# Squares for the norms of queries and keys summed in single passes of TensorE, after GpSimd divides them into a rounded part and a remainder

## What is computed

```python
def l2norm(x):
    return x * lax.rsqrt(jnp.sum(x * x, axis=-1, keepdims=True) + EPS)

q = l2norm(qkv[..., :W].reshape(Bsz, S, H, Dh))
k = l2norm(qkv[..., W:2 * W].reshape(Bsz, S, H, Dh))
```

## Time and profile before

| | us |
|---|---|
| median of 3 runs | 2419.33 (2419.21 to 2419.52) |
| the profiled execution's own time | 2419.28 |
| its span, first to last instruction | 2417.6 |
| TensorE busy with matmuls | 2393.9 |
| VectorE busy | 1613.9 |
| ScalarE busy | 1165.9 |
| GpSimd busy | 158.0 |
| eight sums L1136, modelled length of the 16 entries together (16 x 0.593) | 9.5 |

### The profile page before, as it was taken

The page is one execution under the profiler, slowest core; times in us unless marked ns, Lnnn a source line. Parts: engine busy times, 40 slices in busy tenths (PEclk is TensorE's granted clock), DMA queues, the critical chain, the costliest instruction groups (busy, mean ns, idle before and its releaser), DMA issues.

```text
span 2417.6 us, 35323 instructions
## 1 busy us (share of the span) xinstructions
PE 2393.9 (99%) x14051; PEld 2069.5 (86%) x14051; DVE 1613.9 (67%) x2035; ACT 1165.9 (48%) x1404; POOL 158.0 (7%) x142
## 2 busy tenths in 40 slices
PE   8999999999999999999999999999999999999998
PEld 7888988888888888889988888888888888888887
DVE  6999676556675876697655445455777467755764
ACT  5433674545564654642654344345554344433433
POOL 1000000000200100000000000000222012200220
PEclk9999999999999999999999999999999999999999
DMA  8655446454435555653175554444655555555554
GB/s 250 196 187 196 153 139 226 137 190 157 159 117 195 169 179 176 191 158 106 40 262 177 184 201 147 146 167 145 203 192 190 198 185 187 195 188 195 181 178 144
DMA packets 337349, 422.43 MB, mean 175 GB/s; under 512 B 8494, under 2 KB 263228, under 8 KB 336716
## 3 DMA queue, kind: packets, MB, share of 16 engines
q1 hardware_dynamic: 334220, 410.87, 51.4%
q0 software_dynamic: 2544, 8.52, 1.1%
q10 hardware_dynamic: 464, 1.32, 0.2%
HBM read 418.53 MB, written 2.10 MB: 174 GB/s over the span
## 4 chain that ended last, share of the span: by engine, by line
PE 97%; DVE 2%; ACT 1%; DMA 0%; issue 0%; ACTq 0%; DVEq 0%
PE ps L747 36%; PE ps L748 18%; PE ps L806 10%; PE ps L804 10%; PE ps L805 10%; PE ps L751 1%; PE ps L750 1%; PE ps L752 1%; PE ps L1101 1%; PE ps L1093 1%; PE ps L1314 1%; PE ps L1015 1%; PE ps L1305 1%; PE ps L1018 1%; PE ps L843 0%; DVE h_cat L2285 0%
## 5 line engine op out<-in xcount | busy, mean ns | idle before, releaser
L747 PE MATMUL ps<-h_cat,w_hi 128*128 128x512 f32 x3824 | 1343.2, 396 | 5.6 <-DVE h_cat L2285 4.9
L748 PE MATMUL ps<-h_cat,w_lo 128*128 128x256 f32 x3824 | 1064.7, 278 | 0.0
L747 PEld LDWEIGHTS ps<-h_cat,w_hi 128*128 128x128 f32 x3824 | 716.9, 187 | 176.2 <-issue 7.5
L748 PEld LDWEIGHTS ps<-h_cat,w_lo 128*128 128x128 f32 x3824 | 719.9, 188 | 2.2 <-issue 1.9
L2142 DVE TENSOR_TENSOR w_lo<-ring,w_hi 128x2048 fp32r<-128x2048 f32 (+2 forms) x279 | 588.5, 2112 | 178.6 <-ACT w_hi L1395 175.8
L1395 ACT ACTIVATE w_hi<-ring 128x2048 fp32r<-128x2048 f32 (+2 forms) x279 | 493.1, 1768 | 86.4 <-PE ps L806 63.0
L2138 DVE TENSOR_TENSOR w_lo<-ring,w_hi 128x2048 fp32r<-128x2048 f32 (+1 forms) x136 | 303.1, 2233 | 230.2 <-ACT w_hi L1392 227.4
L1392 ACT ACTIVATE w_hi<-ring 128x2048 fp32r<-128x2048 f32 (+1 forms) x136 | 252.5, 1863 | 271.0 <-PE ps L806 250.4
L804 PE MATMUL ps<-w_hi,h_cat 128*128 128x512 f32 x640 | 250.6, 392 | 0.0
L806 PE MATMUL ps<-w_hi,h_cat 128*128 128x512 f32 x640 | 249.2, 389 | 0.0
L805 PE MATMUL ps<-w_lo,h_cat 128*128 128x512 f32 x640 | 249.0, 389 | 0.0
(11 more groups left out here) (439 smaller groups left out, 2262.6 us busy)
## 6 DMA issues: line engine op xcount, KB each, us to landing
ring<-in_w_ffn_up SPq DMA_DIRECT2D x44, 2048.0 KB, 8.0
ring<-in_w_mix_in SPq DMA_DIRECT2D x28, 2048.0 KB, 8.2
ring<-in_even_w_in SPq DMA_DIRECT2D x27, 2048.0 KB, 8.0
ring<-in_w_ffn_down SPq DMA_DIRECT2D x16, 2048.0 KB, 8.0
ring<-in_odd_w_in SPq DMA_DIRECT2D x11, 2048.0 KB, 9.2
ring<-in_even_w_out SPq DMA_DIRECT2D x8, 2048.0 KB, 8.1
ring<-in_odd_w_out SPq DMA_DIRECT2D x8, 2048.0 KB, 8.3
ring<-in_w_mix_out SPq DMA_DIRECT2D x8, 2048.0 KB, 8.3
```

What stands on the lines that cost most here:

```text
L747: mm(o[:, 0:2 * T], whi[slot][:, k, :], flat(cat[:, k]), start=first, stop=False)
L748: ins = mm(o[:, T:2 * T], wlo[slot][:, k, :], cat[:, k, 0, :], start=False, stop=end)
```

## The change

Each norm gets a step of GpSimd between square and sum. It casts the two halves of l2 into two tiles of the single-pass type, and subtracts them from l2 in place. TensorE waits for this step instead of the square. It sums the remainders (512 columns) and adds the rounded halves (256 columns each) in the same bank, with the ones taken as the single-pass type. One rounded half stands in 1 KB behind the delta rule's tiles, the other in the place of the tile rstd, which is not used then. ScalarE and VectorE are left as they are. The GpSimd steps are queued behind the masks and ahead of the load of L640.

```diff
-            add("act", "l2_square", s), add("pe", "l2_sum", s), add("act", "l2_root", s), add("dve", "l2_scale", s)
+            add("act", "l2_square", s), add("pool", "l2_split", s), add("pe", "l2_sum", s), add("act", "l2_root", s), add("dve", "l2_scale", s)
...
+    RSTD = at[0]
     rstd = place("rstd", [P, T])
...
     l2 = place("l2", [P, 2, T], off=XSQ)
+    l2_hi = [place("l2_hi0", [P, T], F32R, off=AR + 40 * KB), place("l2_hi1", [P, T], F32R, off=RSTD)]
+    l2_lo = place("l2_lo", [P, 2, T], F32R, off=XSQ)
...
+        def l2_split(s):
+
+            after(pool, "l2_square", s)
+            for i in range(2):
+                ch.link(pool.tensor_copy(l2_hi[i][:], l2[:, i, :]))
+            for i in range(2):
+                ins = pool.tensor_tensor(l2_lo[:, i, :], l2[:, i, :], l2_hi[i][:].bitcast(F32), ALU.subtract)
+                if i == 0:
+                    ch.link(ins)
+            return ins
+
+        for s in range(8):
+            l2_split(s).then_inc(sem["gdn_pool"], 1)
         pool.wait_ge(sem["h_ready"], H_GROUPS["gdn"] + 4)
...
         def l2_sum(s):
-            after(pe, "l2_square", s)
-            return mm(ps[4][:], ones[:], l2[:].rearrange("p a t -> p (a t)"), start=True, stop=True)
+            after(pe, "l2_split", s)
+            one = ones[:].bitcast(F32R)
+            mm(ps[4][:], one, flat(l2_lo[:]), start=True, stop=False)
+            mm(ps[4][:, 0:T], one, l2_hi[0][:], start=False, stop=False)
+            return mm(ps[4][:, T:2 * T], one, l2_hi[1][:], start=False, stop=True)
```

More of the change, by code:

```diff
@@ L402, in build @@
              "idx_ready", "relu_ready", "idx_added", "top_ready", "uk_turned", "ukt_ready", "vk_ready", "vk_drained",
-             "qkv_silu", "masks_ready", "gdn_pe", "gdn_act", "gdn_dve", "gdn_loaded",
+             "qkv_silu", "masks_ready", "gdn_pe", "gdn_act", "gdn_dve", "gdn_pool", "gdn_loaded",
              "mem_loaded", "mem_scaled", "ffn_silu", "ffn_prod", "act_ready",
```

## The result

The changed kernel takes 2429.31 us, median of 6 runs (2427.65 to 2431.13), against 2419.43 us (2419.07 to 2420.80, 6 runs): ratio 1.0041, 95% interval 1.0031 to 1.0051. The prediction was 2429.6 us. The profiled execution took 2430.25 us, with a span of 2428.5 us, 10.9 us more than before.

What follows compares the result with a forecast made beforehand. TensorE was taken to bound the kernel, with VectorE nearly full beside the sums. Waits of 13.4 us less 3.1 us saved made 10.3 us longer, 2429.6 us; stated range 2422 to 2437 us, the forecast's own 2427.5 to 2433.

Steps and rivals of the forecast that it cites:

- TensorE has no rest, VectorE little: Around the norm sums: TensorE bounds the run with no rest to give; VectorE is busy 46.74 of 48 us.
- The new sum, 0.47 us, and 3.1 us saved: TensorE's eight norm sums: each takes 0.47 us in place of 0.86, saving 3.1 us, all on the path.
- The split's own length: GpSimd between square and sum: two casts of 0.36 us, two subtractions of 0.70, gaps of 0.07; 2.33 us undisturbed.
- The port excludes: Beside the split: VectorE's L2142, L2161, L2196, L2711 and GpSimd's four instructions wait for each other; L2175 isn't held.
- The first wait, 2.8 us: First norm: one cast gets in, VectorE's next w_lo holds the rest, and TensorE waits 2.8 us.
- Norms 2 to 5: 0.4, 0.8, 0.4 and 0: Norms 2 to 5: w_lo holds the last subtraction; TensorE waits 0.4, 0.8 and 0.4 us, and 0 in norm 5.
- Norms 6 to 8: 3.0 us each: Last three norms (g_h): GpSimd pushes VectorE's full stream by 1.75 us to a 14.58 us period; TensorE waits 3.0 us each.
- The rival of the clock, 0.03: Behind three long waits TensorE's clock falls, one 5.55 us unit each at 1.2 GHz: 16.6 us more, 2446 us; chance 0.03.
- a fall of the granted clock: Sign in the changed profile that would show the prediction wrong: TensorE's granted clock, 1.00 before, falls.

Runs made afterwards that it cites:

- half_reciprocal: Changed kernel, but VectorE takes the reciprocals of one of the two slices and scales both with them; 2422.16 us, ratio 1.0011.
- sum_only: Changed kernel without GpSimd's split: ScalarE writes rounded squares and the three single-pass matmuls sum them twice; 2418.62 us, ratio 0.9997.
- write_only: sum_only plus five linked GpSimd memsets, which read nothing, between square and sum; 2419.10 us, ratio 0.9999.
- after_again: The changed kernel, unaltered, run once more for a second profile; 2428.64 us, ratio 1.0039.
- act_rounds: Changed kernel, but ScalarE writes the rounded halves by squaring a second time and GpSimd only subtracts; 2421.65 us, ratio 1.0010.
- fill_first: Changed kernel with six fp32 matmuls of 256 columns into an unused bank ahead of TensorE's wait for the first split; 2428.02 us, ratio 1.0037.

## Why the prediction was right, point by point

**TensorE has no rest, VectorE little.** Right: every wait came through as time, and half_reciprocal shows that all waits but the first hang on VectorE.

**The new sum, 0.47 us, and 3.1 us saved.** The sum takes 0.47 us, 0.58 behind a wait. That all of the 3.1 us are on the path was too much: sum_only kept 1.1.

**The split's own length.** Casts were put at 0.36 us and take 0.40; subtractions at 0.70 and take 0.72 to 0.74 where nothing holds them; gaps at 0.07 and take 0.06 to 0.09.

**The port excludes.** Right for what reads; write_only shows that GpSimd's memsets are free of it. The sentence that L2175 (now L2195) isn't held is borne out by its 0.41 us. The list of what is held was one short: the multiplication by the first tap (L2158, now L2178) was not in it and takes 0.70 in place of 0.35 us. The kernel before had a row for it, beside GpSimd's cast of 1732.27:

```profile
1732.28 0.75 DVE L2158 TENSOR_SCALAR cvg<-stage,prm 128x256 f32<-128x256 f32 x1 [0.16 <-DVE stage L2175]
```

By the rule of the Trainium skill (SBUF — State Buffer, Who interferes with whom), an instruction that only writes is not in contention with VectorE's two-input ones; by that rule the traces agree, 0.40 us beside w_lo.

**The first wait, 2.8 us.** 2.84 and 2.85 measured, by the step as told: one cast, w_lo, the rest. That w_lo gets in ahead of the second cast was a near tie that went the way the step had it.

**Norms 2 to 5: 0.4, 0.8, 0.4 and 0.** Measured in after_again, where no fall of the clock disturbs them: 0.24, 0.83, 0.24 and 0.

**Norms 6 to 8: 3.0 us each.** This is the term that was mis-sized. The step was that the cast and the two subtractions push VectorE by their whole length, "0.36+0.70+0.70 = 1.75 us", to a period of 14.58. The period is 13.78: they push it by 0.95. VectorE's own instructions grew by 0.21, 0.35 and 0.42 us, 0.98 together, less than the 1.9 us that the three GpSimd ones last (0.40, 0.78 and 0.72). The rows show two reasons. Each VectorE instruction starts when the GpSimd one has already run for a while, 0.04, 0.23 and 0.11 us. And it ends sooner behind the GpSimd one than its own length: L2178, which takes 0.35 us alone, ends at 1079.36, 0.15 us behind the first subtraction (1078.43 + 0.78 = 1079.21). So 0.15 to 0.21 us of each passed under the wait, 0.56 together, and 1.90 - 0.38 - 0.56 = 0.96. That this part is a fixed start-up of the instruction is a reading, not shown. The earlier trace rows had the sign of it: of the 1.2 us that the subtraction of 1733.08 still had to run, L2161 lost some 1.0. TensorE in turn needs 11.88 us between two sums in place of 11.57 (0.1 for the restart, 0.2 for the slower spacing of pairs), so 13.78 - 11.88 = 1.9 us are left. The waits were 1.5, 1.9 and 1.9, or 5.3 us in place of 9.0.

**The rival of the clock, 0.03.** It was told as a unit of 5.55 us at half speed behind each of three long waits, 16.6 us; it came in one profile behind one wait, for half a unit and a sum, 2.9 us, and not in the next. The chance was too low and the price too high. The prediction had named a fall of the granted clock as a sign that it would be wrong, and in the first profile that sign was there.

**What was missing** are small things: the slower spacing of pairs (0.2 us for two units) and the 0.1 us of a restart. In after_again the account is 9.7 of waits, 0.7 of restarts, 1.0 of spacing, less 3.1: 8.3 us, and D grew by 8.33. Its execution took 9.3 us longer than the one before; of the 1.0 us outside D, 0.6 stand ahead of the first sum and belong to no step.

So the number was right by luck in part. 13.4 us of waits were predicted and 9.2 (first profile) and 9.7 (after_again) came. The 3.7 to 4.2 us too much stood against the small terms, 1.3 to 1.7 us, against the clock in the first profile, 2.9 us, and in after_again against what lies outside D, where the number still comes out 1.0 us too high. With 5.3 us in place of 9.0 and no other term changed, the prediction's own sum gives 6.6 us, or 2425.9 us, below the range of its forecast. The sign, the place and the mechanism didn't need the luck.

## What to carry to other kernels

Work that is moved to an idle engine is not free when it stands in a chain with a fixed place on the engine that bounds the kernel: compare its length, with what it waits for at a shared port, with the rest that the chain has at that place, and look at the tightest of its repetitions. A saving on the bound engine counts only as far as the next engine has slack; here VectorE had 0.76 us by the rows, and taking its reciprocals away gave 2.0 us on top of the 1.6 that the shorter sums gave without it. Where work would have to run on GpSimd beside VectorE, a form that doesn't read SBUF (write_only) or ScalarE for part of it (act_rounds, 7.7 us under the changed kernel) cost less here.

## What the runs showed of the hardware that was not expected

- A pair of matmuls (512 and 256 columns) runs at 0.3467 or at 0.3535 us, in long stretches at the full clock, and changes from one to the other at breaks in the stream. In the kernel before it changed at about 975 us and kept the faster one through all eight fp32 sums.
- A wait of 2.85 us let TensorE's granted clock fall to 0.50 in one profile of the changed kernel and left it at 1.00 in another; in fill_first it fell behind one of 2.1 us, and in after_again one of 2.1 us left it at 1.00.
- The first matmul behind a wait takes 0.1 us more until the next starts (0.34 in place of 0.23).
- Of VectorE's instructions of 0.35 to 0.49 us beside GpSimd's readers, each lost 0.2 to 0.4 us to one of 0.4 to 0.8 us.
